# Weight loads issued from GpSimd's queue instead of SyncE's

## The chip, the cores and the metric

The kernel runs on one core of one Trainium2 chip. Five engines take part: TensorE (PE in the profile; PEld are its weight loads), VectorE (DVE), ScalarE (ACT), GpSimd (POOL) and SyncE (SP). Each has its own queue of instructions, worked off in order; semaphores tie the queues together. A transfer is issued by an instruction in one of these queues and then runs on the core's 16 DMA engines. The metric is the time of one execution on the device, in microseconds; lower is better.

## What is computed

One inference step of a one-layer streaming encoder, on 1024 prompt tokens and 8 x 16 sample tokens of width 1024, in fp32:

```
x = x + 0.5 * SwiGLU_1(RMSNorm(x))                 # 1024 -> 2816 -> 1024
z = RMSNorm(x) @ w_in                              # 1024 -> 2500 columns: q, k, v, indexer
A = differential attention, 4 heads                # softmax(q0 k0) - lam * softmax(q1 k1)
B = sparse attention, 8 heads, one shared key and value; an indexer picks the top 256 keys
x = x + concat(A, B) @ w_out
x = x + 0.5 * SwiGLU_2(RMSNorm(x))
```

Queries and keys are RMS-normalised by head. The outputs are x and the new keys and values of prompt and samples.

## The kernel before

**Tiling.** The nine tiles of 128 tokens form two groups: GA (prompt tiles 0 to 3 and the sample tile) and GB (prompt tiles 4 to 7). Each weight matrix is passed over once for each group. The stages in order of time are: FFN 1 of GA (from 26 us), FFN 1 of GB, with the norm and projection of GA in it (from about 510), the sample's attention and the attention of GA beside the rest of FFN 1 of GB (from about 710), out-projection of GA and projection of GB (from about 1376), FFN 2 of GA beside the attention of GB (from about 1590), out-projection of GB and its norm (from about 2265), and FFN 2 of GB alone (from about 2410).

**Weights.** The weights come in 160 loads of 1 MB (four of them 904 KB) into `raw`, a ring of `RAW = 2` slots. A gate or up load is 128 partitions x 8 x 256 floats, so 1024 pieces of 1 KB; a load of `w_in` or `w_out` is 512 pieces of 2 KB; one of `w_down` is 256 pieces of 4 KB. Each load is used as two units. ScalarE copies a unit to `w_hi` (L1452), rounded to the format of the fast matmul; DVE computes `w_lo = raw - w_hi` (L1735); both lie in rings of `HILO = 4`. TensorE multiplies three times (L1150 to L1152 for gate and up, L1167 to L1169 for down, L1187 to L1189 for the projections). `load(n)` waits until DVE has split the last unit of load n - 2 (`w_ready`), and its landing raises `raw_loaded`, which ScalarE's split waits for (named L2270 in the profile).

**The order.** `make_plan` writes one list of items by hand-set weights; every engine walks the whole list and issues its own part of each item. `Plan` puts `("load", n + 2)` right behind the split that frees the slot. So the order of each queue is fixed at build time.

**SyncE** issues every transfer: the loads; x tiles (`load_x`, L2277) and norm gains; the projection's results (`p_finish`, L2331), four stores a tile in its last column group; the key, query, value and bias tiles of attention (`k_store` L2383, `keys` L2395, `q_load` L2423, `near` L2415); attention rows for the out-projection (`o_load`, L2358), which wait until the buffer of two is free; and the outputs.

**GpSimd** does little: it writes constants at the start, then turns each sum of squares into a factor by two short operations, a scaled sum and a power of -0.5. These are `mean` and `rstd` for the norms (L2207, L2209; DVE's scaling into `rows`, L1811, waits for them), `p_mean` and `p_rstd` for the heads of a projection (L2216, L2218; DVE's `p_rows` waits), and `omean` and `orstd` for the heads of differential attention (L2228, L2230; DVE's `o_store` waits). It also clears some tiles with memsets (L2234, L2235). At the start, each x tile goes through ScalarE's square, GpSimd's two operations, DVE's `rows`, TensorE's transposes (L1207) and a copy and difference into `XTh` and `XTl`, before the first split.

Of the kernel before, what the change touches and what calls it, by code (L numbers as in the profile page):

```python
# [28 lines left out]
P = 128  # L29
D = 1024  # L30
KD = D // P
# [10 lines left out]
F_PAIR = 2  # L42
# [20 lines left out]
OUT_GROUP = 512  # L63
# [68 lines left out]
F_PAIR = 2  # L132
# [5 lines left out]
IN_GROUPS = -(-IN_COLS // OUT_GROUP)  # L138
TAIL = IN_COLS - (IN_GROUPS - 1) * OUT_GROUP
# [3 lines left out]
PAIRS = tuple((ffn, g, f) for ffn in range(2) for g in range(2) for f in range(N_PAIR))  # L143
HILO, RAW = 4, 2
# [573 lines left out]
def build(nc, io):  # L718
    plan = Plan()
# [11 lines left out]
    with ExitStack() as ctx:  # L731
# [12 lines left out]
        raw = sb("raw", [P, RAW, 2 * D])  # L744
# [9 lines left out]
        with ExitStack() as layout:  # L754
# [6 lines left out]
            with ExitStack() as shared:  # L761
# [4 lines left out]
                square = lay_s("square", [P, D], F16)  # L766
# [147 lines left out]
        w_ready = sem("w_ready")  # L914
# [215 lines left out]
        with nc.Block() as block:  # L1130
# [1062 lines left out]
            def _(pool):  # L2193
                order = Chain(pool, pool_chain)

                def start():
                    pool.memset(ident[:], 0.0).then_inc(ident_zero, 1)
                    pool.memset(mhalf[:], -0.5).then_inc(mhalf_set, 1)
                    pool.wait_ge(ident_zero, 1)
                    pool.affine_select(out=ident[:], in_=ident[:], compare_op=ALU.not_equal, fill=1.0, base=0,  # L2200
                                       pattern=[[-1, P]], channel_multiplier=1).then_inc(ident_ready, 1)
                    pool.wait_ge(mhalf_set, 1)

                def square_rows(tag, i):
# [32 lines left out]
                def x_norm(part):  # L2237
                    if part == 1:
# [3 lines left out]

                stages = {"start": start, "square": square_rows, "mm": mm, "near_zero": near_zero, "o_square": o_square,
                          "x_begin": x_begin, "x_norm": x_norm}
# [5 lines left out]
            def _(sp):  # L2250
                def load(n):
                    name = plan.loads[n]
                    if n >= RAW:
                        sp.wait_ge(w_ready, plan.load_end[n - RAW] + 1)
                    slot = raw[:, n % RAW]
                    if name[0] == "gu":
                        _, p, w = name
                        ffn, g, f = PAIRS[p]
                        src = (wu if w else wg)[ffn][:, :, f * F_PAIR * P:(f + 1) * F_PAIR * P]
                        dst = slot.rearrange("p (k n) -> p k n", k=KD)  # L2260
                    elif name[0] == "d":
                        ffn, g, f = PAIRS[name[1]]
                        src = wd[ffn][:, f * F_PAIR:(f + 1) * F_PAIR, :]
                        dst = slot.rearrange("p (k n) -> p k n", k=2)
                    else:
                        phase, g, cg, half = name
                        width = TAIL if phase == "P" and cg == IN_GROUPS - 1 else OUT_GROUP
                        src = (w_in if phase == "P" else w_out)[:, 4 * half:4 * half + 4, cg * OUT_GROUP:cg * OUT_GROUP + width]
                        dst = slot.rearrange("p (k n) -> p k n", k=4)[:, :, 0:width]
                    sp.dma_start(dst, src).then_inc(raw_loaded[n % RAW], 16)  # L2270

                def load_x(g, i):
# [6 lines left out]
                def start():  # L2279
# [3 lines left out]
                    load_x(GA, 2)  # L2283
                    load(0)
                    load_x(GA, 3)
                    load(1)
                    load_x(GA, 4)
# [223 lines left out]
                def past_sample():  # L2511
                    sp.wait_ge(s_stored, 32)
                    sp.sem_inc(fence, 1)

                stages = {"start": start, "load": load, "gain": gain, "tab": tab, "tab_store": tab_store, "p_finish": p_finish,
                          "spill": spill, "enter": enter, "reload": reload, "o_load": o_load, "down": down, "k_load": k_load,
# [45 lines left out]
```

## Time and profile before

| What | Value |
|---|---|
| Median of 3 runs | 2785.19 us (2785.16 to 2785.62) |
| The profiled execution | 2782.92 us, around a span of 2781.1 us |
| PE, DVE, ACT, POOL busy | 2553.6, 1456.4, 1061.2, 136.4 us |
| Granted TensorE clock, mean | 0.966 of full speed |
| Moved by DMA | 271.29 MB, 98 GB/s in the mean, all of the kernel's transfers on one queue (q1) |
| Weight loads | 160, 1024 KB each, about 5 us from issue to landing |

The profile shows one execution. "Idle before" is the time in which an engine had nothing running ahead of an instruction, and the arrow names what ended it. SPq rows are instructions that issue a transfer on SyncE; their duration is that of the issue, not that of the transfer. TensorE's matmuls overlap, so that the busy times of single rows add up to more than the stretch they stand in.

### The profile page before, as it was taken

The page shows a single profiled execution, that of the slowest core. Times are in us where ns is not written, and L with a number is a line of the kernel's source. Part 1 is how long each engine was busy: PE and PEld are TensorE (multiplying, and loading weights), DVE is VectorE, ACT ScalarE, POOL GpSimd, SP SyncE. Part 2 cuts the span into 40 slices and gives each one's busy share as a digit, 9 for nine tenths or more (in the row PEclk, how much of TensorE's full clock was granted, in tenths as well). Part 3 has the DMA queues.
Part 4 walks back from the last instruction along what each step waited for, and adds up shares of the span by engine and source line. Part 5 has one row for each costly group of instructions (what it writes and reads, how often), then busy time and mean ns, then how long its engine had stood idle before and what let it go on. Part 6 is the DMA issues. An engine that isn't in the chain of part 4 may idle for free.

```text
span 2781.1 us, 36356 instructions
## 1 busy us (share of the span) xinstructions
PE 2553.6 (92%) x13547; PEld 2181.6 (78%) x13547; DVE 1456.4 (52%) x2884; ACT 1061.2 (38%) x1821; POOL 136.4 (5%) x203
## 2 busy tenths in 40 slices
PE   7999999999899977878799997888899989999997
PEld 6899999888677666666688886778788878888886
DVE  4445444543454347875445358878755534444443
ACT  3132222332332235644334347775545532222221
POOL 0000000122000000000003100000000000000000
PEclk9999999999999998998899999999999999999998
DMA  5231221323533342222333442222112122322321
GB/s 179 78 119 62 90 76 61 137 102 122 156 129 112 99 137 89 86 72 76 118 122 120 156 128 70 72 79 79 59 47 64 56 94 99 114 91 95 103 91 61
DMA packets 244076, 271.29 MB, mean 98 GB/s; under 512 B 72096, under 2 KB 196544, under 8 KB 243904
## 3 DMA queue, kind: packets, MB, share of 16 engines
q1 hardware_dynamic: 243904, 268.98, 29.6%
q8 instruction: 110, 1.80, 0.3%
q14 instruction: 62, 0.51, 0.1%
HBM read 235.21 MB, written 35.29 MB: 97 GB/s over the span
## 4 chain that ended last, share of the span: by engine, by line
PE 70%; DVE 10%; issue 7%; ACT 7%; DMA 3%; SPq 1%; DVEq 0%; POOL 0%; ACTq 0%
PE bank L1150 10%; PE bank L1151 10%; PE bank L1152 10%; PE bank L1167 5%; PE bank L1168 5%; PE bank L1169 5%; PE bank L1187 4%; PE bank L1189 4%; PE bank L1188 4%; PE bank L1277 2%; ACT w_hi L1452 2%; DVE w_lo L1735 2%; PE bank L1412 1%; ACT junk_a_b L1609 1%; PE bank L1207 1%
## 5 line engine op out<-in xcount | busy, mean ns | idle before, releaser
L1735 DVE TENSOR_TENSOR w_lo<-raw,w_hi 128x1024 fp32r<-128x1024 f32 x320 | 385.8, 1219 | 194.1 <-ACT w_hi L1452 194.0
L1150 PE MATMUL bank<-XTh_a,w_hi 128*128 128x320 f32 x1408 | 449.1, 319 | 22.4 <-DVE act_in L1748 19.5
L1151 PE MATMUL bank<-XTl_a,w_hi 128*128 128x320 f32 x1408 | 441.1, 313 | 0.0
L1152 PE MATMUL bank<-XTh_a,w_lo 128*128 128x320 f32 x1408 | 441.0, 313 | 0.0
L1452 ACT ACTIVATE w_hi<-raw 128x1024 fp32r<-128x1024 f32 x320 | 330.1, 1046 | 171.1 <-PE bank L1189 105.7
L1167 PE MATMUL bank<-w_hi,hid_hi 128*128 128x512 f32 x792 | 325.2, 411 | 13.9 <-DVE X_a L1766 10.7
L1168 PE MATMUL bank<-w_lo,hid_hi 128*128 128x512 f32 x792 | 315.0, 398 | 0.0
L1169 PE MATMUL bank<-w_hi,hid_lo 128*128 128x512 f32 x792 | 313.8, 396 | 0.0
L1150 PEld LDWEIGHTS bank<-XTh_a,w_hi 128*128 128x128 f32 x1408 | 270.6, 192 | 34.9 <-issue 14.5
L1150 PE MATMUL bank<-XTh_b,w_hi 128*128 128x512 f32 x704 | 293.2, 416 | 0.0
L1151 PE MATMUL bank<-XTl_b,w_hi 128*128 128x512 f32 x704 | 284.0, 403 | 0.0
L1152 PE MATMUL bank<-XTh_b,w_lo 128*128 128x512 f32 x704 | 283.9, 403 | 0.0
L1766 DVE SCALAR_TENSOR_TENSOR X_a<-bank,X_a 128x512 f32<-128x512 f32 x220 | 151.6, 690 | 239.5 <-PE bank L1169 236.8
L1151 PEld LDWEIGHTS bank<-XTl_a,w_hi 128*128 128x128 f32 x1408 | 270.8, 192 | 5.3
L1152 PEld LDWEIGHTS bank<-XTh_a,w_lo 128*128 128x128 f32 x1408 | 270.0, 192 | 0.0
L1465 ACT ACTIVATE act_in<-bank 128x320 f32<-128x320 f32 (+1 forms) x132 | 64.8, 491 | 413.2 <-PE bank L1152 400.0
L1766 DVE SCALAR_TENSOR_TENSOR X_b<-bank,X_b 128x512 f32<-128x512 f32 x176 | 121.5, 691 | 179.0 <-PE bank L1169 175.8
L1470 ACT ACTIVATE hid_hi<-act_in 128x320 fp32r<-128x320 f32 (+1 forms) x132 | 69.1, 523 | 351.8 <-DVE act_in L1748 351.6
L1167 PEld LDWEIGHTS bank<-w_hi,hid_hi 128*128 128x128 f32 x792 | 151.1, 191 | 48.6 <-issue 20.8
L1169 PEld LDWEIGHTS bank<-w_hi,hid_lo 128*128 128x128 f32 x792 | 151.3, 191 | 34.6
L1168 PEld LDWEIGHTS bank<-w_lo,hid_hi 128*128 128x128 f32 x792 | 151.7, 192 | 25.5
L1152 PEld LDWEIGHTS bank<-XTh_b,w_lo 128*128 128x128 f32 x704 | 135.9, 193 | 33.6
(314 smaller groups left out, 3938.8 us busy)
## 6 DMA issues: line engine op xcount, KB each, us to landing
raw<-in_w_gate SPq DMA_DIRECT2D x44, 1024.0 KB, 5.0
raw<-in_w_up SPq DMA_DIRECT2D x44, 1024.0 KB, 5.0
raw<-in_w_down SPq DMA_DIRECT2D x44, 1024.0 KB, 4.8
raw<-in_w_in SPq DMA_DIRECT2D x16, 1024.0 KB, 4.8
s_k_in<-in_cache_diff_k SPq DMA_DIRECT2D x16, 512.0 KB, 4.7
s_v_in<-in_cache_diff_v SPq DMA_DIRECT2D x8, 1024.0 KB, 5.6
raw<-in_w_out SPq DMA_DIRECT2D x8, 1024.0 KB, 5.1
q_rows_b<-q_scr SPq DMA_DIRECT2D x80, 64.0 KB, 2.2
```

The source lines that it names most:

```text
L1150: pe.matmul(out, hi[:, k], XTh[g][:, k, lo:up], start=(k == 0), stop=False)
L1151: pe.matmul(out, hi[:, k], XTl[g][:, k, lo:up], start=False, stop=False)
L1152: last = pe.matmul(out, low[:, k], XTh[g][:, k, lo:up], start=False, stop=(k == KD - 1))
L1167: pe.matmul(out_of(key)[:], hid_hi[:, j, tok], hi[:, j], start=(j == 0), stop=False)
L1168: pe.matmul(out_of(key)[:], hid_hi[:, j, tok], low[:, j], start=False, stop=False)
L1169: last = pe.matmul(out_of(key)[:], hid_lo[:, j, tok], hi[:, j], start=False, stop=(j == F_PAIR - 1))
L1187: pe.matmul(out, XTh[g][:, k, tok], hi[:, e], start=(k == 0), stop=False)
L1188: pe.matmul(out, XTh[g][:, k, tok], low[:, e], start=False, stop=False)
L1189: last = pe.matmul(out, XTl[g][:, k, tok], hi[:, e], start=False, stop=(k == KD - 1))
L1452: act.activation(hilo(w_hi, u)[:, :, 0:width_of(u)], raw_part(u), ACT.Copy).then_inc(w_hi_ready, 1)
L1735: dve.tensor_tensor(hilo(w_lo, u)[:, :, 0:width_of(u)], raw_part(u), hilo(w_hi, u)[:, :, 0:width_of(u)].bitcast(F32), ALU.subtract).then_i ...
L1766: dve.scalar_tensor_tensor(x, out_of(key)[:], 0.5, x, ALU.mult, ALU.add).then_inc(frees(key), 1)
```

## The change

The function `load` and its 160 calls move from the SyncE program to the GpSimd program. Nothing else is changed: not the sizes, the semaphores, the ring of two slots or the places in the list of items. In GpSimd's `start`, loads 0 and 1 stand behind the constants; on SyncE they stood between the x tiles.

```diff
             @block.gpsimd
                 def start():
...
                     pool.wait_ge(mhalf_set, 1)
-
+                    load(0)
+                    load(1)
+
+                def load(n):
+                    name = plan.loads[n]
+                    if n >= RAW:
+                        pool.wait_ge(w_ready, plan.load_end[n - RAW] + 1)
+                    slot = raw[:, n % RAW]
...
+                    pool.dma_start(dst, src).then_inc(raw_loaded[n % RAW], 16)
...
+                stages = {"start": start, "load": load, "square": square_rows, "mm": mm, "near_zero": near_zero, "o_square": o_square,
             @block.sync
-                def load(n):
-                    name = plan.loads[n]
-                    if n >= RAW:
-                        sp.wait_ge(w_ready, plan.load_end[n - RAW] + 1)
...
-                    sp.dma_start(dst, src).then_inc(raw_loaded[n % RAW], 16)
...
                     load_x(GA, 2)
-                    load(0)
                     load_x(GA, 3)
-                    load(1)
                     load_x(GA, 4)
...
-                stages = {"start": start, "load": load, "gain": gain, "tab": tab, "tab_store": tab_store, "p_finish": p_finish,
+                stages = {"start": start, "gain": gain, "tab": tab, "tab_store": tab_store, "p_finish": p_finish,
```

GpSimd's queue at the end of the projection of GA, before (`p_mean` and `p_rstd` of the last column group for the last three of five tiles, then the two memsets of the sample's attention):

```order
L2216 TENSOR_SCALAR p_mean<-p_sum 128x1
L2218 TENSOR_TENSOR p_rstd<-p_mean,mhalf 128x1
L2216 TENSOR_SCALAR p_mean<-p_sum 128x1
L2218 TENSOR_TENSOR p_rstd<-p_mean,mhalf 128x1
L2234 MEMSET s_qi 128x512
L2235 MEMSET s_qm 128x1280
L2240 TENSOR_SCALAR s_ossum<-s_ossum 128x4
L2241 TENSOR_TENSOR s_orstd<-s_ossum,mhalf 128x4
```

And in the changed kernel:

```order
L2225 DMA raw<-in_w_up 128x8x256
L2239 TENSOR_SCALAR p_mean<-p_sum 128x1
L2241 TENSOR_TENSOR p_rstd<-p_mean,mhalf 128x1
L2239 TENSOR_SCALAR p_mean<-p_sum 128x1
L2241 TENSOR_TENSOR p_rstd<-p_mean,mhalf 128x1
L2239 TENSOR_SCALAR p_mean<-p_sum 128x1
L2241 TENSOR_TENSOR p_rstd<-p_mean,mhalf 128x1
L2225 DMA raw<-in_w_gate 128x8x256
L2257 MEMSET s_qi 128x512
L2258 MEMSET s_qm 128x1280
```

Two weight loads have come in between: one ahead of the third of the five pairs, one ahead of the memsets.

SyncE's queue before the out-projection of GB, before (`o_scr` is where attention leaves its rows, `rows` the buffer of two from which they are transposed, `x_scr` the stored x):

```order
L2270 DMA raw<-in_w_out 128x4x512
L2433 DMA o_scr<-o_b 128x128 x2
L2352 DMA X_b<-x_scr 128x1024 x4
L2358 DMA rows<-o_scr 128x1024 x3
L2270 DMA raw<-in_w_out 128x4x512
L2358 DMA rows<-o_scr 128x1024
L2270 DMA raw<-in_w_out 128x4x512
L2270 DMA raw<-in_w_gate 128x8x256
L2270 DMA raw<-in_w_down 128x2x1024
```

And in the changed kernel:

```order
L2433 DMA o_scr<-o_b 128x128 x6
L2352 DMA X_b<-x_scr 128x1024 x4
L2358 DMA rows<-o_scr 128x1024 x4
L2306 DMA gain_b<-in_g_ffn 128x1024
L2367 DMA out_y_p<-X_a 128x1024 x4
```

The loads of `w_out` have left the row, so the four transfers to `rows` now follow each other directly.

## Rows read from the trace of the kernel before

**Rows 1.** Page, parts 1 and 4: engines busy; chain that ended last.

```profile
PE 2553.6 (92%) x13547; PEld 2181.6 (78%) x13547; DVE 1456.4 (52%) x2884; ACT 1061.2 (38%) x1821; POOL 136.4 (5%) x203
...
PE 70%; DVE 10%; issue 7%; ACT 7%; DMA 3%; SPq 1%; DVEq 0%; POOL 0%; ACTq 0%
```

**Rows 2.** Tile `raw`: idle us, waits, what ended them; issue to landing.

```profile
  DMA raw<-in_w_down: 10.7, 1
...
DMA to landing us min/median/max: 4.4/5.0/11.1
```

**Rows 3.** Waits of SyncE's own queue: us in total, times, longest.

```profile
SPq L2270 <- DVE w_lo L1735: 1450.4, 152, 22.9
```

**Rows 4.** Timeline, last stage: start, us, engine and operation, [idle before].

```profile
2570.25 0.37 SPq L2270 DMA_DIRECT2D raw<-in_w_down  x1
2584.57 0.37 SPq L2270 DMA_DIRECT2D raw<-in_w_up  x1
...
2574.42 2.00 ACT L1452 ACTIVATE w_hi<-raw 128x1024 fp32r<-128x1024 f32 x2
...
2595.34 1.05 ACT L1452 ACTIVATE w_hi<-raw 128x1024 fp32r<-128x1024 f32 x1
...
2580.92 0.69 DVE L1748 TENSOR_TENSOR act_in<-act_in,bank 128x512 f32<-128x512 f32 x1 [2.64 <-PE bank L1152]
```

**Rows 5.** Groups of GpSimd: count, busy us, mean ns of one.

```profile
L2235 POOL MEMSET s_qm<- 128x1280 f32 x1 | 1.2, 1164 | 0.0
```

**Rows 6.** Timeline, end of the first projection: ScalarE, DVE, GpSimd, SyncE.

```profile
693.43 1.06 ACT L1452 ACTIVATE w_hi<-raw 128x1024 fp32r<-128x1024 f32 x1 [10.73 <-DMA raw<-in_w_down]
...
698.39 1.23 DVE L1735 TENSOR_TENSOR w_lo<-raw,w_hi 128x1024 fp32r<-128x1024 f32 x1 [0.73 <-ACT w_hi L1452]
...
700.30 0.19 POOL L2216 TENSOR_SCALAR p_mean<-p_sum 128x1 f32<-128x1 f32 x1 [1.72 <-DVE p_sum L1782]
...
700.11 0.55 SPq L2331 DMA_DIRECT2D out_sk_p<-p_rows  x1
700.69 0.43 SPq L2331 DMA_DIRECT2D out_sv_p<-p_rows  x1
```

**Rows 7.** Timeline, the start: GpSimd and DVE.

```profile
1.16 0.29 POOL L2200 TENSOR_SCALAR_AFFINE_SELECT ident<-ident 128x128 f32<-128x128 f32 x1 [0.20 <-POOL ident L2197]
...
5.69 0.19 POOL L2207 TENSOR_SCALAR mean<-ssum 128x1 f32<-128x1 f32 x1 [4.24 <-ACT square L1503]
...
19.83 1.28 DVE L1811 SCALAR_TENSOR_TENSOR rows<-X_a,rstd,gain_b 128x1024 f32<-128x1024 f32 x1
...
24.74 1.23 DVE L1735 TENSOR_TENSOR w_lo<-raw,w_hi 128x1024 fp32r<-128x1024 f32 x1 [0.25 <-ACT w_hi L1452]
```

**Rows 8.** Timeline near 2275: TensorE, SyncE; landing of the transfers to tile `rows`.

```profile
2273.09 1.47 PE L1207 MATMUL bank<-ident,rows 128*128 128x128 f32 x12
...
2282.16 1.12 PE L1207 MATMUL bank<-ident,rows 128*128 128x128 f32 x4 [7.60 <-DMA rows<-o_scr]
...
2276.46 0.51 SPq L2358 DMA_DIRECT2D rows<-o_scr  x1
...
DMA to landing us min/median/max: 3.1/5.7/9.5
```

**Rows 9.** Timeline, key stores of group A: DVE, SyncE, TensorE.

```profile
1021.04 0.69 DVE L1867 CAST k_out_a<-bank 128x512 fp32r<-128x512 f32 x1
...
1025.88 3.56 SPq L2383 DMA_DIRECT2D kT_scr<-k_out_a  x2
...
1038.81 0.69 PE L1246 MATMUL bank<-kT_a,q_hi_a 128*128 128x384 f32 x1 [8.64 <-DMA kT_a<-kT_scr]
```

**Rows 10.** Timeline near 1095: DVE and GpSimd.

```profile
1094.80 1.23 DVE L1735 TENSOR_TENSOR w_lo<-raw,w_hi 128x1024 fp32r<-128x1024 f32 x1 [0.26 <-ACT w_hi L1452]
1098.75 0.34 DVE L1979 SCALAR_TENSOR_TENSOR o_a<-o_a,orstd_a,sub_gain 128x128 f32<-128x128 f32 x1
...
1095.14 0.93 POOL L2228 TENSOR_SCALAR omean_a<-ossum_a 128x1 f32<-128x1 f32 x1 [10.16 <-ACT o_sq_a L1597]
```

More of the change, by code:

```diff
@@ L2202, in start @@
                     pool.wait_ge(mhalf_set, 1)
+                    load(0)
[5 more added lines that the diff above has]
+                    slot = raw[:, n % RAW]
+                    if name[0] == "gu":
+                        _, p, w = name
+                        ffn, g, f = PAIRS[p]
+                        src = (wu if w else wg)[ffn][:, :, f * F_PAIR * P:(f + 1) * F_PAIR * P]
+                        dst = slot.rearrange("p (k n) -> p k n", k=KD)
+                    elif name[0] == "d":
+                        ffn, g, f = PAIRS[name[1]]
+                        src = wd[ffn][:, f * F_PAIR:(f + 1) * F_PAIR, :]
+                        dst = slot.rearrange("p (k n) -> p k n", k=2)
+                    else:
+                        phase, g, cg, half = name
+                        width = TAIL if phase == "P" and cg == IN_GROUPS - 1 else OUT_GROUP
+                        src = (w_in if phase == "P" else w_out)[:, 4 * half:4 * half + 4, cg * OUT_GROUP:cg * OUT_GROUP + width]
+                        dst = slot.rearrange("p (k n) -> p k n", k=4)[:, :, 0:width]
+                    pool.dma_start(dst, src).then_inc(raw_loaded[n % RAW], 16)
                 def square_rows(tag, i):
@@ L2241, in x_norm @@
                         pool.tensor_tensor(s_orstd[:], s_ossum[:], mhalf[:, 0:DIFF_HEADS], ALU.pow).then_inc(s_orstd_ready, 1)
-                stages = {"start": start, "square": square_rows, "mm": mm, "near_zero": near_zero, "o_square": o_square,
+                stages = {"start": start, "load": load, "square": square_rows, "mm": mm, "near_zero": near_zero, "o_square": o_square,
                           "x_begin": x_begin, "x_norm": x_norm}
@@ L2250, in _ @@
             def _(sp):
-                def load(n):
-                    name = plan.loads[n]
-                    if n >= RAW:
-                        sp.wait_ge(w_ready, plan.load_end[n - RAW] + 1)
[L2255 to L2269, printed above, removed]
-                    sp.dma_start(dst, src).then_inc(raw_loaded[n % RAW], 16)
                 def load_x(g, i):
```

## The prediction

> **What bounds the kernel now.** I read the profile from the top down. TensorE is busy for 92% of the span and makes up 70% of the chain that ended last [rows 1]. DMA is 3% of that chain, the SyncE queue 1%, GpSimd almost nothing. So the kernel is bound by TensorE, and a change of queues can only move the 227 us (2781.1 - 2553.6) in which TensorE stands idle.
>
> The second view is the one of the weight tile: of all 320 splits that read `raw`, one waited for its transfer, for 10.7 us; a load lands 5.0 us after its issue in the median and 11.1 us at worst [rows 2]. The loads are prefetched well, and what they cost SyncE's queue is head-of-line time: the queue stood for 1450 us before weight loads, waiting for `w_lo` [rows 3]. Other transfers stand behind such a wait. GpSimd, which takes the loads over, is busy for 5% of the span [rows 1]. Its short operations feed DVE (`rstd`, `p_rstd`, `orstd`), and they will now stand behind loads in the same way.
>
> So there are three questions: which transfers come earlier on SyncE, which GpSimd operations come later, and whether a load issued by GpSimd lands late.
>
> **The unknown: what a load costs on GpSimd.** No DMA is issued there in this trace, so I bound the time g for which one gate or up load (1024 pieces of 1 KB) holds the engine. From below: SyncE issues it in 0.37 us [rows 4]. Above it, what is unknown is the work of listing the pieces: 1024 pieces with a source and a destination each are 2048 entries, and GpSimd's own memset takes 1.16 us for 1280 columns, 0.91 ns a column [rows 5]; at one column's time an entry that is 1.9 us. As the upper end I take four columns' time an entry, 7.5 us. I take g = 2 us, because a memset is the nearest row of work that only writes; half of it for `w_in` and `w_out` (512 pieces), a quarter for `w_down` (256). A gain below 0.37 us is excluded, since SyncE's issue writes nothing itself. The landing moves by about as much: +2 us for gate and up, +0.5 us for `w_down`, if the list is finished before the data moves; 0 to +7.5 us at the ends.
>
> **Late landing.** The tightest loads are the `w_down` of the last stage. One is issued at 2570.25, lands about 5 us later, and ScalarE splits it as the second of two `w_hi` from 2574.42 [rows 4], so at 2575.4: under half a microsecond of room, at some ten places. Behind it DVE has 2.64 us of idle time before its product at 2580.92 [rows 4], so +0.5 us is hidden, and up to about 3 us would be. The next up load is issued at 2584.57 and split at 2595.34 [rows 4], 10.8 us later, so it may land 5.8 us late. Cost: 0. The one landing that was waited for is the `w_down` split at 693.43 [rows 6], in the tail of a projection; there +0.5 us goes through at worst. If g is 7.5, it is 1.9 us.
>
> A rule of the Trainium skill speaks against the change (page "DMA: Bandwidth & Descriptors", section "Measured (HBM→SBUF, 128 partitions, SWDGE, issued from GpSimd)"): 1 MB issued from GpSimd keeps the DMA engines 6.15 us, whereas the whole way from issue to landing is 5.0 us here [rows 2]. By it every landing would come one to two microseconds later still, and the sum would stay, because the room named above is 3 us.
>
> **The start.** Now the five x tiles and two weight loads share one queue, and the first `w_lo` starts at 24.74 [rows 7]. With the loads elsewhere, issued from 1.45 (the end of `affine_select`, [rows 7]), GpSimd is blocked until S = 1.45 + 2g. Its first `mean` runs at 5.69, so g = 2 (S = 5.45) delays nothing. From S on, the chain needs 0.85 us for mean and power, 1 us to the first `rows`, five tiles at 2.66 us of DVE (1.28 for `rows` [rows 7], about 0.69 for each of two `XTl`), and about 2 us of latency: 17.2 us. At g = 2 it is done by 22.6 instead of 24.5: gain 1.9 us if the tiles come early enough, which they should, for 2 of the 5 MB ahead of the last one leave its queue, though not the DMA engines. Bounds: +10 us cost at g = 7.5 (S = 16.5, done by 33.7, minus 24.5), 3 us gain below.
>
> **SyncE freed.** Three places matter. (a) The last load of attention rows for group B. TensorE does twelve transposes from 2273.09; the fourth frees the buffer by about 2273.6. SyncE stands before a `w_out` load and issues `rows` right behind it, at 2276.46 [rows 8], with its 1 MB ahead; TensorE waits 7.60 us for it, until 2282.16 [rows 8]. In the changed kernel it is issued 2.9 us earlier and lands in about 3.1 us, the best of its group, instead of 5.7 [rows 8]. Gain 2.9 to 5.5 us; I take 5, as the weight load then starts only when the rows have landed. (b) The key stores of group A: the part whose cast starts at 1021.04 is stored only at 1025.88, right behind a weight load, and TensorE waits 8.64 us at 1038.81 for what follows [rows 9]. The last part is ready only at about 1026 anyway, so only bandwidth is gained: 0 to 3 us, taken as 1. (c) Elsewhere (query rows behind a gate load near 1038, the store burst at 700 to 710 with two loads of 0.4 us in it, rows behind `w_out` near 1388) single waits of 2 us or so shrink: 0 to 3 us, taken as 1.5. Sum 9.4 us.
>
> A second page rule is weighed here. The Trainium skill, same page, section "Issuing engines are not separate DMA queues", says that issuing from several engines saves only the sequencer's time, as all run on the same 16 DMA engines. The row at 2276.46 speaks for more: there the queue's order, not the issue, costs 2.9 us. By the rule the sum would lose the landing part of (a) and all of (b), about 3 us.
>
> **GpSimd's own operations.** Every one that stands behind a load in the new order is delayed by g plus the remaining wait for `w_lo`; what counts is when DVE needs the result. Near 700 the last three `p_mean` stand behind an up load that is ready at 699.6, when `w_lo` from 698.39 ends; the first ran at 700.30 and would start at 701.6 [rows 6]. DVE is 1.3 us late. But SyncE stores these tiles from 700.11 on, four transfers of about 0.5 us each a tile [rows 6], and reaches the third tile at about 704, when its data is 2.5 us old: no cost. Near 1095 DVE's `w_lo` ends at 1096.03, so `orstd` is ready at 1096.8 + g; DVE uses it at 1098.75 [rows 10]. That leaves 1.9 us: cost g - 1.9. There are four more such places (`orstd` near 1108, 1164 and 1772, `rstd` near 2344), with 1.6 to 4 us of room. At g = 2 they sum to about 1.5 us, and I add 0.3 for the split at 693.43 and small stalls. At g = 5 they cost 4 + 3 + 3 + 2 + 3.4 = 15 us.
>
> **Sum.** -9.4 + 1.8 = -7.6 us against the profiled execution (2782.92 us around a span of 2781.1). The median of the three runs is 2785.19, 2.3 us above that execution; so 2785.2 - 7.6 = 2777.6, about **2778 us**.
>
> **Rivals.**
> 1. *Listing the pieces is slow and GpSimd becomes a gate.* Same mechanism with g = 5: the start costs S = 11.45, done by 28.7, so 4.2 us instead of a gain of 1.9; the delayed results cost 15; the load split at 693.43 and small stalls 1.5 to 3; the up loads of the last stage land 5 us late and have 5.8. The gains of SyncE stay at 7.5. Net +15: 2800 us. It decides from g = 3.4, where costs equal gains. For it: 1024 small pieces a load. Against it: GpSimd is nearly empty. At g = 7.5 it is 2825.
> 2. *GpSimd and DVE get in each other's way.* The `omean` at 1095.14 took 0.93 us while DVE ran `w_lo`, and the `mean` at 5.69 took 0.19 [rows 7, 10]; so the two do disturb each other where both read SBUF. If a load's issue waits for DVE or holds it for its 2 us, 160 loads meet DVE in half of the cases (it is busy 52%, [rows 1]); with TensorE covering three quarters of that, it costs 160 x 0.5 x 2 x 0.25 = 40 us: 2818 us. The Trainium skill (page "SBUF — State Buffer", section "Who interferes with whom") says that DVE's `tensor_tensor` takes only the read side of the shared ports, and that descriptors need the write side; by that this rival falls.
> 3. *It does nothing:* the same bytes on the same DMA engines, loads that nobody waits for, and the freed places are caught by the next wait (the chain near 1038 and 2282 has other feeders). 2785 us.
> 4. *All gains at their ends, g near 0.4:* -3 - 5.5 - 3 - 3 = -14.5: 2771 us.
>
> **Chances.** Forecast 0.42, rival 1 0.28, rival 2 0.08, rival 3 0.14, rival 4 0.08. A measurement of this kernel tells 0.2% (5.6 us) from no change, so faster means below 2779.6. The forecast's own spread of 4 us puts about 0.27 of its 0.42 below that and 0.15 within; rival 4 is all faster; rival 3 and a fifth of rival 1 are within. That makes 0.35 faster, 0.35 same and 0.30 slower. The range runs from rival 4 to g of about 6.5: 2771 to 2815.
>
> **What would show each step.** `DMA` rows of GpSimd with g in them, against 2 us. The first `w_lo` at about 22.8. TensorE's wait of 7.60 us before the rows near 2282 falls to about 2.5. SyncE's waits for `w_lo` are gone, and GpSimd has them. The wait for `raw` stays near one. If DVE shows new waits for `orstd`, `p_rstd` or `rstd`, rival 1 holds; if `w_lo` itself takes longer than 1.22 us, rival 2. The forecast is wrong if g is over 3.4, or if the waits at 1038 and 2282 stay.

## The result, and the profile after

The changed kernel is faster, by more than forecast: 2769.03 us in the median of five runs (2766.69 to 2772.28), beside 2785.16 us for the kernel before (2782.32 to 2785.62, five runs). The ratio is 0.9944, 95% interval 0.9930 to 0.9959. The prediction was 2778 us with a range of 2771 to 2815; the measured time lies 2 us below it. The profiled execution took 2766.69 us around a span of 2764.1, so 17.0 us less than the one of before.

The first lines of the page (busy time and share of each engine, then the chain that ended last) and part 3 of the page (queues: packets, MB, share of the 16 engines):

```profile
PE 2545.1 (92%) x13547; PEld 2174.5 (79%) x13547; DVE 1456.3 (53%) x2884; ACT 1061.6 (38%) x1821; POOL 268.0 (10%) x363
...
q0 software_dynamic: 43200, 167.29, 17.4%
q1 hardware_dynamic: 125632, 101.69, 11.5%
...
PE 70%; DVE 10%; issue 7%; ACT 7%; DMA 3%; SPq 1%; POOL 0%; DVEq 0%; ACTq 0%
```

TensorE's busy time fell from 2553.6 [rows 1] to 2545.1, by 8.5 us, with the same 13547 matmuls. The idle time fell from 227.5 to 219.0 us (span minus busy), also by 8.5. So half of the gain between these two traces is no waiting time at all: the same matmuls spent less time at the lower granted clock. The mean granted clock of the changed kernel's five executions is 0.968 to 0.972, 0.970 in the mean, beside 0.966 for 21 executions of the kernel before. (The 0.972 of the profiled one reads too high: at the start its trace gives 1.00 where the matmuls run as slowly as before, 0.47 us for 320 columns.) The prediction has no term for the clock.

The second view is GpSimd's: its groups of instructions (line, operation, tiles, count | busy us, mean ns of one), and the longest of its waits (us, times, longest).

```profile
L2225 POOL DMA_DIRECT2D raw<-in_w_up x44 | 40.7, 924 | 778.1 <-DVE w_lo L1735 778.1
L2225 POOL DMA_DIRECT2D raw<-in_w_gate x44 | 39.6, 901 | 317.7 <-DVE w_lo L1735 317.5 <-issue 0.2
L2225 POOL DMA_DIRECT2D raw<-in_w_down x44 | 31.9, 724 | 627.2 <-DVE w_lo L1735 627.2
```

```profile
POOL raw L2225 <- DVE w_lo L1735: 2013.8, 157, 38.0
```

A load holds GpSimd for 0.9 us (gate and up) or 0.7 us (`w_down`), where g was taken as 2 us. SyncE's 1450 us of waiting for `w_lo` [rows 3] are gone, and GpSimd waits instead. The tile view of `raw`, on who waited for its transfer and on landing times:

```profile
  DMA raw<-in_w_down: 13.7, 7
...
DMA to landing us min/median/max: 4.9/5.5/15.4
```

A load lands 5.5 us after its issue, not 5.0 [rows 2]. Seven splits waited for a transfer where it was one, for 13.7 us in all instead of 10.7.

Now the places. At the start (GpSimd, then DVE, then ScalarE's square of the last x tile; start, us, operation, [idle before]):

```profile
1.70 1.03 POOL L2225 DMA_DIRECT2D raw<-in_w_gate  x1 [0.24 <-issue]
2.73 0.89 POOL L2225 DMA_DIRECT2D raw<-in_w_up  x1
```

```profile
8.48 2.48 DVE L1811 SCALAR_TENSOR_TENSOR rows<-X_a,rstd,gain_b 128x1024 f32<-128x1024 f32 x2 [6.58 <-DMA gain_b<-in_g_ffn]
...
24.22 4.63 DVE L1735 TENSOR_TENSOR w_lo<-raw,w_hi 128x1024 fp32r<-128x1024 f32 x4 [0.25 <-ACT w_hi L1452]
```

```profile
16.44 1.06 ACT L1503 ACTIVATE square<-X_a 128x1024 bf16<-128x1024 f32 x1 [0.57 <-DMA X_a<-in_x_sample]
```

In the kernel before, the same square:

```profile
16.96 1.06 ACT L1503 ACTIVATE square<-X_a 128x1024 bf16<-128x1024 f32 x1 [1.89 <-DMA X_a<-in_x_sample]
```

The first `w_lo` starts at 24.22 instead of 24.74 [rows 7]. The last x tile is issued at 3.07 instead of 5.31, but it lands only 0.5 us earlier. Before the last attention rows (SyncE, then TensorE), and TensorE's row in the table of stretches for the 4 us behind that wait (busy and count of PE, PEld, DVE, ACT, POOL; clock; DMA share; GB/s):

```profile
2265.20 0.32 SPq L2358 DMA_DIRECT2D rows<-o_scr  x1
```

```profile
2268.51 1.09 PE L1207 MATMUL bank<-ident,rows 128*128 128x128 f32 x8 [2.47 <-DMA rows<-o_scr]
```

```profile
2268.00:2272.00 4.00, 3.49 (x26) 3.49 (x27) 3.44 (x6) 1.09 (x2) 0.51 (x1) 1.00 0.97 327
```

The wait is 2.47 us instead of 7.60 [rows 8], and the clock stays at 1.00. In the kernel before, the stretch behind the same wait reads 0.50, the lower of the two levels (1.2 GHz):

```profile
2282.00:2286.00 4.00, 3.84 (x16) 3.84 (x17) 1.38 (x2) 1.19 (x2) 0.00 (x0) 0.50 0.00 0
```

At the key stores of group A (SyncE, TensorE):

```profile
1019.87 4.60 SPq L2383 DMA_DIRECT2D kT_scr<-k_out_a  x2
```

```profile
1032.71 0.69 PE L1246 MATMUL bank<-kT_a,q_hi_a 128*128 128x384 f32 x1 [4.46 <-DMA kT_a<-kT_scr]
```

The wait of 8.64 us [rows 9] is 4.46. The kernel before has a second one behind it, for query rows, which the changed kernel has not:

```profile
1046.38 0.44 PE L1232 MATMUL bank<-ident,q_rows_a 128*128 128x128 f32 x2 [2.14 <-DMA q_rows_a<-q_scr]
```

The same place of group B is worse than before (GpSimd, SyncE, TensorE):

```profile
1600.60 0.92 POOL L2225 DMA_DIRECT2D raw<-in_w_up  x1 [22.66 <-DVE w_lo L1735]
```

```profile
1600.96 2.21 SPq L2383 DMA_DIRECT2D kT_scr<-k_out_b  x2
```

```profile
1616.84 0.47 PE L1246 MATMUL bank<-kT_b,q_hi_b 128*128 128x128 f32 x1 [9.10 <-DMA kT_b<-kT_scr]
```

TensorE waits 9.10 us here, 5.82 in the kernel before, whose SyncE issued the same load and the same two stores so:

```profile
1610.22 0.38 SPq L2270 DMA_DIRECT2D raw<-in_w_up  x1
1610.85 3.22 SPq L2383 DMA_DIRECT2D kT_scr<-k_out_b  x2
...
1624.74 0.48 PE L1246 MATMUL bank<-kT_b,q_hi_b 128*128 128x128 f32 x1 [5.82 <-DMA kT_b<-kT_scr]
```

The landing times of tile `kT_scr`, for group A (issues of 1020 to 1030 in the kernel before, of 1015 to 1026 in the changed one), then for group B (1610 to 1615 before, 1600 to 1604 changed):

```profile
DMA to landing us min/median/max: 8.3/8.9/9.5
```

```profile
DMA to landing us min/median/max: 3.3/3.4/3.5
```

```profile
DMA to landing us min/median/max: 7.4/7.9/8.4
```

```profile
DMA to landing us min/median/max: 9.3/9.5/9.7
```

In group A the stores now get away before the weight load and land in 3.4 us. In group B the load stood just ahead of two stores in the kernel before (by 0.6 us) and still does (by 0.4 us), now on the other queue: the stores land after 9.5 us instead of 7.9, so the queue of its own does not shield them. DVE's cast that makes these stores ready starts at 1600.22 instead of 1610.11, so 9.9 us earlier; TensorE's first matmul on the keys starts only 7.9 us earlier. These 2.0 us are what the transfers cost more than before. At 1600, however, TensorE was 12.4 us ahead of the kernel before. The other 2.5 us of that lead the cast never shared.

The two traces hold the same matmuls in the same order. The lead of the changed kernel at a given matmul is its start before minus its start after, and how it grows over a stretch is what that stretch gained. The table has this for the changed kernel and for experiments of the next section (each against the same trace of the kernel before):

```
                         lead gained, us, from..to (time in the kernel before)
                         start   keys A         keys B         last rows      all
                         ..26.0  1020.3..1060.2 1600.2..1660.0 2265.1..2300.1 ..2768.1
changed kernel            0.5     7.5           -4.4            6.6           17.0
e1 five loads on GpSimd   0.0     7.4           -1.9            6.9           14.2
e2 the other 155          1.5     0.9           -4.0            0.3           -1.1
e11 SyncE waits again     1.1     3.8           -3.9            2.9            0.6
e4 hold                   1.4     8.9            1.4            5.8           20.1
e3 order alone           -0.1    11.0            4.9            6.0           24.6
e5 w_out load later       0.1    -0.5            1.7            6.7            9.7
e6 two loads of A later   0.0    11.1           -0.6            0.1           11.3
```

Stretches whose code an experiment leaves alone show the scatter of one trace: up to 1.7 us in the table (e5, keys B), and from 26 to 1020, which the table leaves out, e3, e5 and e6 lost 2.0 to 2.5 us.

### The profile page after: what moved, and what is told of

It is laid out like the page before. It is cut to its first block, busy times and chain, and to the rows that moved or that the text cites. A ratio compares the mean times of both kernels' runs of the same rounds, so it can differ in the third digit from the quotient of the medians.

```text
span 2764.1 us, 36355 instructions
## 1 busy us (share of the span) xinstructions
PE 2545.1 (92%) x13547; PEld 2174.5 (79%) x13547; DVE 1456.3 (53%) x2884; ACT 1061.6 (38%) x1821; POOL 268.0 (10%) x363
## 3 DMA queue, kind: packets, MB, share of 16 engines
q0 software_dynamic: 43200, 167.29, 17.4%
q1 hardware_dynamic: 125632, 101.69, 11.5%
## 4 chain that ended last, share of the span: by engine, by line
PE 70%; DVE 10%; issue 7%; ACT 7%; DMA 3%; SPq 1%; POOL 0%; DVEq 0%; ACTq 0%
PE bank L1150 10%; PE bank L1151 10%; PE bank L1152 10%; PE bank L1167 5%; PE bank L1168 5%; PE bank L1169 5%; PE bank L1187 4%; PE bank L1189 4%; PE bank L1188 4%; PE bank L1277 2%; ACT w_hi L1452 2%; DVE w_lo L1735 2%; PE bank L1412 1%; ACT junk_a_b L1609 1%; PE bank L1369 1%
## 5 line engine op out<-in xcount | busy, mean ns | idle before, releaser
L1735 DVE TENSOR_TENSOR w_lo<-raw,w_hi 128x1024 fp32r<-128x1024 f32 x320 | 386.2, 1219 | 194.6 <-ACT w_hi L1452 194.4
L1167 PE MATMUL bank<-w_hi,hid_hi 128*128 128x512 f32 x792 | 324.4, 410 | 13.2 <-DVE X_a L1766 10.7
```

What stands on the lines that cost most here:

```text
L1167: pe.matmul(out_of(key)[:], hid_hi[:, j, tok], hi[:, j], start=(j == 0), stop=False)
L1735: dve.tensor_tensor(hilo(w_lo, u)[:, :, 0:width_of(u)], raw_part(u), hilo(w_hi, u)[:, :, 0:width_of(u)].bitcast(F32), ALU.subtract).then_i ...
```

## The experiments

The kernel before was run beside each of three groups of experiments and took 2781.79, 2781.29 and 2784.53 us. So ratios are compared, and the time of its own group stands behind "before" each time.

### Is it a few places, or all 160 loads?

e1 issues five loads from GpSimd: 62 and 63 (group A), 94 and 95 (group B), which stand between key stores, keys and query rows, and 121, which stands before the last attention rows. e2 is the complement. The loads of either queue count on semaphores of their own.

```diff
+    ON_POOL = {62, 63, 94, 95, 121}          # e2: set(range(160)) - {62, 63, 94, 95, 121}
...
                 def load(n):                  # in the GpSimd program
+                    if n not in ON_POOL:
+                        return
...
                 def load(n):                  # in the SyncE program
+                    if n in ON_POOL:
+                        return
```

> The kernel before, with five of its 160 loads issued from GpSimd: the two up and two gate loads that stand between the key stores, key loads and query rows at the opening of either group's attention (numbers 62, 63, 94, 95), and the w_out load in front of the last attention rows (121). The other 155 stay on SyncE. Theory (the gain is the place of a few loads in SyncE's queue): the key chain of group A starts as early as in the changed kernel, TensorE's wait of 8.64 us at 1038.81 falls to about 4.5, the wait of 7.60 us at 2282.16 goes, together 13 us of the 17: 2772 us. In group B the stores still run into an up load on the shared DMA engines, so nothing is gained there. Rival (the gain is spread: smaller issue cost on SyncE, fewer and larger packets for all 160 loads): 5 of 160 loads move a thirtieth of it: 2784 us.

Measured: 2769.70 us (2768.87 to 2770.95), before 2781.79; ratio 0.9955 (0.9942 to 0.9967).

> The complement: those five loads stay where they were in SyncE's queue, the other 155 are issued from GpSimd. Theory: the waits of TensorE at the opening of group A's attention (8.64 us) and before the last attention rows (7.60 us) stay; what is left is the start (0.5 us) and single small stalls: 2781 us. Rival (spread gain): nearly all of it, 2769 us.

Measured: 2785.65 us (2781.97 to 2790.02), before 2781.79; ratio 1.0016 (1.0007 to 1.0025). TensorE's waits for keys and for rows, in e2's timeline:

```profile
1036.48 0.69 PE L1248 MATMUL bank<-kT_a,q_hi_a 128*128 128x384 f32 x1 [10.08 <-DMA kT_a<-kT_scr]
...
2283.39 0.90 PE L1209 MATMUL bank<-ident,rows 128*128 128x128 f32 x3 [7.62 <-DMA rows<-o_scr]
```

Five loads bring 12 of the 16 us. The other 155 bring nothing, and the interval says that they cost a little, some 4 us. By the table e2 loses 4.0 us at the keys of B, where its loads are on SyncE as before: it came there 3.1 us ahead, the key stores were issued no earlier than before, and the lead was gone. The two parts together (0.9955 x 1.0016 = 0.9971) are less than the whole (0.9944); what the remaining 0.27% are stays open. The theory of places stands, the rival of a spread gain falls.

### Each place by itself, without GpSimd

e5 and e6 keep all loads on SyncE and only move them in its order. A load item is skipped in the walk through the plan and issued behind another item:

```diff
+                moved = {("load", 121): ("o_load", "otb", 3)}      # e5
+                moved = {("load", 62): ("q_load", 4), ("load", 63): ("q_load", 6)}      # e6
                 for item in plan.items:
-                    if item[0] in stages:
+                    if item[0] in stages and item not in moved:
                         stages[item[0]](*item[1:])
+                    for load_item, anchor in moved.items():
+                        if item == anchor:
+                            load(load_item[1])
```

> The kernel before; in SyncE's order the w_out load 121 stands behind the last attention rows instead of in front of them, nothing else. Theory (the 17 us are three places, each by itself): TensorE's wait of 7.60 us at 2282.16 shrinks to about 2, and the clock, which fell to 0.50 behind that wait, stays at 1.00, worth 1.5 us more: 2.9 + 4 us, about 6.5 in all, 2775 us beside 2782 for before. Rival (the earlier rows only move the wait to the next feeder): under 2 us, 2780.

Measured: 2774.37 us (2771.14 to 2780.15), before 2781.29; ratio 0.9979 (0.9970 to 0.9988). The page's first line and the wait:

```profile
PE 2548.7 (92%) x13547; PEld 2177.5 (79%) x13547; DVE 1455.4 (53%) x2884; ACT 1060.9 (38%) x1821; POOL 136.6 (5%) x203
```

```profile
2275.87 1.09 PE L1207 MATMUL bank<-ident,rows 128*128 128x128 f32 x8 [2.44 <-DMA rows<-o_scr]
```

> The kernel before; only loads 62 and 63 stand later in SyncE's order, behind the query rows of block 4 and of block 6 of group A. Theory: TensorE's 8.64 us at 1038.81 fall to 4 or less and the query rows at 1046.38 are no longer late: 8 to 9 us, 2773 us beside 2782 for before. Rival (the term of my prediction was right, 1 us for the bandwidth and some for the rows; the rest came from elsewhere): 2 to 3 us, 2779.

Measured: 2772.75 us (2771.65 to 2775.79), before 2781.29; ratio 0.9970 (0.9960 to 0.9981).

```profile
1034.73 0.44 PE L1246 MATMUL bank<-kT_a,q_hi_a 128*128 128x384 f32 x1 [2.08 <-DMA kT_a<-kT_scr]
```

Both came out as the theory had them, 7 and 8.5 us. Each place pays by itself. e5 moved one instruction: its wait shrank by 5.2 us, and its stretch gained 6.7. Part of the rest is the clock: behind the wait it is granted 1.00 (2275 to 2283), where the kernel before reads 0.50.

### The order alone, all three places

e3 moves the same five loads as e1, but in SyncE's order (94 behind `("q_load", 40)`, 95 behind `("q_load", 42)`).

> No load on GpSimd. The same five loads stay on SyncE, only later in its order: the up load behind all key stores, key loads and query rows of block 4, the gate load behind the query rows of block 6 (in both groups), the w_out load behind the last attention rows. Theory (order alone is enough, and it also keeps the 1 MB off the DMA engines while the keys travel): the gain of e1, and in group B more, as the key stores there no longer land after 8 us but after 3.5, and TensorE's 5.82 us at 1624.74 shrink to about 2: 2766 us, faster than the changed kernel. Rival (a queue of their own is what helps, since urgent transfers then don't line up behind 1 MB in one ring): order alone gives only the earlier issue, 2780 us.

Measured: 2758.15 us (2756.96 to 2763.80), before 2781.79; ratio 0.9917 (0.9903 to 0.9930). TensorE at the keys of A, of B, and at the last rows:

```profile
1034.41 0.45 PE L1246 MATMUL bank<-kT_a,q_hi_a 128*128 128x384 f32 x1 [2.15 <-DMA kT_a<-kT_scr]
...
1608.78 0.48 PE L1246 MATMUL bank<-kT_b,q_hi_b 128*128 128x128 f32 x1 [2.06 <-DMA kT_b<-kT_scr]
...
2259.37 0.88 PE L1207 MATMUL bank<-ident,rows 128*128 128x128 f32 x6 [2.42 <-DMA rows<-o_scr]
```

No queue of their own was needed, and by the two ratios (0.9917 and 0.9944) the result is 0.27%, 7.5 us, better than the changed kernel. Group B's keys gain 4.9 us where the changed kernel lost 4.4. The rival (a ring of their own helps) falls.

### Is it the load beside the key stores?

e4 is the changed kernel in which loads 62 and 94 wait longer, until the first three key transfers of their group have landed:

```diff
                 def load(n):                  # in the GpSimd program
...
+                    if n in (62, 94):
+                        m = 2 if n == 62 else 12
+                        pool.wait_ge(keys_loaded[m % K_RING], keys_in[m])
```

> The changed kernel, where GpSimd's loads 62 and 94 (with 63 and 95 queued behind them) also wait until the first three rows of keys of the group have landed. Theory (what is left in the changed kernel is the load's 1 MB on the same 16 DMA engines beside the key stores: 9.66 and 9.27 us to landing in group B against 3.36 and 3.51 in group A): TensorE's wait of 9.10 us at 1616.84 falls to about 3, the one at 1032.71 from 4.5 to about 2.5: 2761 us. Rival (the stores of group B are slow because of their own traffic, 1 MB of rows and values ahead of them): no change, 2769 us.

Measured: 2761.43 us (2758.87 to 2762.84), before 2781.79; ratio 0.9924 (0.9911 to 0.9936). Landing of the two key stores of group B (issues of 1602 to 1606), and TensorE:

```profile
DMA to landing us min/median/max: 3.3/4.0/4.6
```

```profile
1612.86 0.48 PE L1246 MATMUL bank<-kT_b,q_hi_b 128*128 128x128 f32 x1 [3.28 <-DMA kT_b<-kT_scr]
```

The two stores land after 3.3 and 4.6 us instead of 9.7 and 9.3, and TensorE waits 3.28 us instead of 9.10. The forecast of 2761 was met. What held the stores up in group B was the load's 1 MB on the DMA engines at their moment; group B gains 1.4 us here where the changed kernel lost 4.4. Loads 62 and 94 were issued 9.8 and 13.7 us later than they could have been, and still landed 10 and 8 us before their first use.

### The wait in SyncE's queue, or the 1 MB in its ring?

e11 is the changed kernel; SyncE waits again for `w_lo` wherever a load stood, and issues nothing.

```diff
             @block.sync
+                def load(n):
+                    if n >= RAW:
+                        sp.wait_ge(w_ready, plan.load_end[n - RAW] + 1)
...
-                stages = {"start": start, "gain": gain,
+                stages = {"start": start, "load": load, "gain": gain,
```

> The changed kernel, but SyncE still waits for w_lo at each place where a load stood, and issues nothing there. It parts the two things that the change takes from SyncE's queue: the wait in front of other transfers, and the 1 MB ahead of them in one ring. Theory (the wait is the larger part near the last attention rows: it is held from 2273.6 to 2276.0; at the key stores the first store again comes 4 us late, and then runs beside the load): the 6.6 us of the last rows shrink to 2, the 8 us of group A's keys to 3: 2779 us. Rival (it is the shared ring, behind whose 1 MB the rows line up): most of the gain stays, 2771.

Measured: 2781.70 us (2778.97 to 2784.36), before 2784.53; ratio 0.9991 (0.9982 to 1.0000). SyncE and TensorE before the last rows:

```profile
2278.52 0.32 SPq L2358 DMA_DIRECT2D rows<-o_scr  x1
```

```profile
2281.83 1.97 PE L1207 MATMUL bank<-ident,rows 128*128 128x128 f32 x8 [4.77 <-DMA rows<-o_scr]
```

Of the 16 us, 3 are left. It is the wait in front of other transfers that the change took away. What stands ahead of the rows matters too: they are issued late again, but 0.27 us ahead of GpSimd's `w_out` load (2278.79) and not 0.43 us behind it. They land in 3.3 us, so TensorE waits 4.77 us and not 7.60, and that stretch keeps 2.9 of its 6.6 us.

### The cost side: a longer hold of GpSimd

e7 and e12 put work behind each load on GpSimd, on a small tile of its own (three powers, or one). The load is not later, GpSimd's other results are.

```diff
                     pool.dma_start(dst, src).then_inc(raw_loaded[n % RAW], 16)
+                    for _ in range(REPS):      # 3 in e7, 1 in e12
+                        order.link(pool.tensor_tensor(spin[:], spin[:], mhalf[:], ALU.pow))
```

> The changed kernel, where GpSimd computes three powers of a small tile of its own behind each load (about 1.5 us each), so that a load holds it for 5.5 us instead of 0.9, while the load itself is not later. It measures the cost side of the prediction, which had the delayed results cost 15 us at g = 5 and the start 4 instead of a gain of 2. Theory (the costs were sized rightly, only g was not): 15 to 22 us above the changed kernel, 2786 us. Rival (the waits for GpSimd's results were priced too high, since DVE has other work in the gap): under 8 us, 2776.

Measured: 2815.24 us (2814.19 to 2816.09), before 2781.29; ratio 1.0121 (1.0106 to 1.0137). The added work took 1.70 us each, so the hold was 0.9 + 5.1 = 6.0 us. DVE's waits for GpSimd (us, times, longest):

```profile
DVE p_rows L1797 <- POOL p_rstd L2246: 39.0, 29, 6.1
DVE rows L1813 <- POOL rstd L2237: 28.2, 8, 13.5
DVE o_a L1981 <- POOL orstd_a L2258: 21.2, 8, 5.1
```

> As e7, with one power behind each load instead of three: a load holds GpSimd for 2.6 us. Without it the changed kernel took 2769 us, with three 2815 (46 us for 5.2 us of hold). Theory (places have different room, 1.6 to 4 us, so that the first two microseconds of hold are nearly free and the cost rises later, as in the prediction): 2774 us. Rival (cost in proportion): 2784 us.

Measured: 2780.89 us (2776.97 to 2783.39), before 2784.53; ratio 0.9985 (0.9976 to 0.9994).

Both expectations missed, on the same side; e12 lies nearer to its rival. The hold costs from the start: from 0.9944 (hold 0.9) to 0.9985 (2.6) and 1.0121 (6.0), that is 0.24% and then 0.40% for each microsecond, or 6.7 and 11 us. The five places with 1.6 to 4 us of room were not all that pay. In the changed kernel DVE waits for `p_rstd` for 26.0 us, 2.1 at most, where before it was 25.3, and for `orstd` for 1.5. e7 adds 13 us to the first and 26 to the second, and has 28.2 us for `rstd` in eight places; e12 has 9.0 us for `rstd` in three. Of the 50 us between the traces of e7 and of the changed kernel, 24 arise from 1060 to 1600, and 5.4 at the start. By these three points the gain is used up at a hold of about 3.0 us; the prediction had 3.4.

### More of the same order, and GpSimd on top

e8 has e3's order, and in addition loads 0 and 1 behind all x tiles of group A, load 51 behind the sample's first rows, load 78 behind the third attention rows of group A, and each group's reload of X behind its first two attention rows. e9 puts the reloads behind the fourth and third rows and load 78 behind the fifth. e10 is e9 with the 151 loads that were not moved on GpSimd.

```diff
+                moved = {("reload", 0): ("o_load", "ota", 1), ("reload", 1): ("o_load", "otb", 1),   # e9: 3, 2
+                         ("load", 62): ("q_load", 4), ("load", 63): ("q_load", 6), ("load", 94): ("q_load", 40),
+                         ("load", 95): ("q_load", 42), ("load", 121): ("o_load", "otb", 3),
+                         ("load", 51): ("x_new_load", 1), ("load", 78): ("o_load", "ota", 2)}   # e9: 4
...
                     load_x(GA, 2)
-                    load(0)
                     load_x(GA, 3)
-                    load(1)
                     load_x(GA, 4)
+                    load(0)
+                    load(1)
```

> All loads on SyncE, with the order of e3 and more of the same: the first two loads behind all five x tiles of group A; the gate load 51 behind the first rows and keys of the sample stage; the w_out load 78 behind the third attention rows of group A; the reload of X (5 and 4 transfers of 512 KB) behind the first two attention rows of each group instead of in front of them. Theory (every large transfer in front of one that TensorE waits for costs its own time on the DMA engines): start 2 to 3 us, sample stage 2, TensorE's waits for rows of 9.45 and 6.04 us down by 5 and 3: 12 us below e3, 2746 us. Rival (X is needed as soon as the rows, and the start is bound by the gain vector): 2755 us.

Measured: 2748.39 us (2746.02 to 2750.82), before 2781.29; ratio 0.9882 (0.9869 to 0.9896). This is the fastest of all, 1.2% below the kernel before, with no transfer on GpSimd. By the same comparison of matmuls as in the table it gained 3.7 us at the start, 11.2 and 5.1 at the keys and 6.9 at the last rows, 36.4 in all. Beyond e3, most of that is the start and the first attention rows of group B, for which the reload of X no longer stands ahead. TensorE and the rows of group A:

```profile
1361.65 1.09 PE L1207 MATMUL bank<-ident,rows 128*128 128x128 f32 x8 [1.52 <-DMA rows<-o_scr]
1371.69 1.12 PE L1207 MATMUL bank<-ident,rows 128*128 128x128 f32 x4 [6.68 <-DMA rows<-o_scr]
1379.07 0.66 PE L1207 MATMUL bank<-ident,rows 128*128 128x128 f32 x4 [1.05 <-DMA rows<-o_scr]
```

> All loads on SyncE, as in e8, but the reload of X stands behind the fourth attention rows of group A and the third of group B, and the w_out load 78 behind the fifth rows. In e8 the wait for the first rows of group A went, and 6 of the 8 us gained there were given back when the third to fifth rows landed after 9 to 10 us, with the reload and load 78 beside them. Theory: they are kept: 2742 us. Rival (X is now late for the sums that need it): 2750.

Measured: 2752.27 us (2749.40 to 2754.11), before 2784.53; ratio 0.9885 (0.9871 to 0.9898). Not better than e8: the rival. The reload only moved its collision to the next rows. In group A that changed little, 8.2 us of waits beside 9.3:

```profile
1362.23 1.09 PE L1207 MATMUL bank<-ident,rows 128*128 128x128 f32 x8 [1.70 <-DMA rows<-o_scr]
1366.54 0.66 PE L1207 MATMUL bank<-ident,rows 128*128 128x128 f32 x4 [0.93 <-DMA rows<-o_scr]
1369.64 0.66 PE L1207 MATMUL bank<-ident,rows 128*128 128x128 f32 x4 [0.63 <-DMA rows<-o_scr]
1377.09 1.11 PE L1207 MATMUL bank<-ident,rows 128*128 128x128 f32 x4 [4.97 <-DMA rows<-o_scr]
```

In group B the reload now stands ahead of the last rows, and the stretch "last rows" gains 2.1 us instead of 6.9. TensorE there in e9, then in e8:

```profile
2250.29 1.11 PE L1207 MATMUL bank<-ident,rows 128*128 128x128 f32 x4 [6.18 <-DMA rows<-o_scr]
```

```profile
2245.01 3.21 PE L1207 MATMUL bank<-ident,rows 128*128 128x128 f32 x16 [2.50 <-DMA rows<-o_scr]
```

My reason for it (X needed too soon) was wrong: the wait is for rows again.

> The order of e9, with the nine loads that were moved (0, 1, 51, 62, 63, 78, 94, 95, 121) on SyncE and the other 151 on GpSimd. Theory (GpSimd's queue brings nothing of its own; the bytes share the same DMA engines, landings are 0.5 us later, and SyncE's other waits matter nowhere): 2742 to 2747, level with e9 or a little slower, as e2 was with the kernel before. Rival (SyncE's waits for w_lo still hold single transfers, which then come out): 2737.

Measured: 2754.65 us (2753.57 to 2756.11), before 2784.53; ratio 0.9894 (0.9879 to 0.9909). The intervals of e9 and e10 overlap almost fully. With the order right, GpSimd's queue has nothing left to give.

## Why the prediction was right and wrong, point by point

**What bounds the kernel.** Right: TensorE; a change of queues works on its waits. Wrong was the next sentence, that it can *only* move the 227 us of idle time. TensorE's busy time moved as much as its idle time, 8.5 us each. The rows at 2282 and 2268 show one case of it: 0.50 of full clock behind a wait of 7.60 us, 1.00 behind one of 2.47. In e3 busy time is 2544.4 us, in e2 it is 2556.6. By the stretches of the table, busy time fell by 1.2 us at the keys of A and by 1.5 at the last rows, and rose by 0.9 at the start; 3.3 of the fall lie between the keys of A and of B. The rest was not tied to a wait. 1.6 of it are one stretch near 2757, where the trace before reads 0.50 (2757 to 2760) and the changed one, at the same matmuls, 1.00; e3 and e5 show that gain and e1 and e6 do not, so it is scatter.

**The cost of a load on GpSimd.** g was 0.9 us, not 2: mis-sized, but inside the bounds (0.37 to 7.5). I took the row of a memset as the nearest, at one column's time for each of 2048 entries. 1024 pieces took 0.90 us and 256 took 0.70, so that the count hardly matters. The landing moved by 0.5 us instead of 2.

**Late landing.** Right in its result (0): seven splits waited, 13.7 us of ScalarE, but TensorE's lead did not shrink in the last stage (15.4 us at 2300.1, 17.0 at the end). The rule from the Trainium skill (page "DMA: Bandwidth & Descriptors", section "Measured (HBM→SBUF, 128 partitions, SWDGE, issued from GpSimd)"), weighed there, keeps the DMA engines busy for 6.15 us with 1 MB from GpSimd; here the whole way to landing took 5.5 us in the median, 4.9 at least, so the measurement is below the rule.

**The start.** -1.9 forecast, -0.5 measured. GpSimd was free at 3.62 and cost nothing; the step that failed was "if the x tiles come early enough". The two loads shared the DMA engines with x tiles and gain vector: DVE's first `rows` started at 8.48 instead of 7.53, and the last x tile, issued 2.2 us earlier, landed 0.5 us earlier. e8, where the loads stand behind the x tiles, gained 3.7. The bounds were loose as well: the chain cannot start before `mean` at 5.69, so by these figures the gain is at most 1.7 us at any g, not 1.9 or 3, and the cost at g = 7.5 is 9.2 us, not 10.

**(a) The last attention rows.** Right mechanism: 5 us forecast, 6.6 measured, 5.1 of them in the wait and the rest the clock behind it. e5 has it with one instruction moved.

**(b) The key stores of group A.** This is the term of the sum that failed: 1 us forecast. The stretch gained 7.5: 4.2 in the wait for the keys, which is (b) itself, 1.9 where the wait of 2.14 us for query rows is gone, and 1.4 behind that, where the clock reads 1.00 (1038.9 to 1043) and in the kernel before 0.69 (1045 to 1050). The last two belong to (c), which had 1.5 for all of its places. I saw that the last part is ready only at about 1026 and concluded that only bandwidth was to be gained. But the transfer beside the load was the price: two stores took 8.9 us to land behind the load and 3.4 us ahead of it, and all keys wait for the last store. The rows to read were the landings of the stores near 1025, and I had taken none.

**Group B's keys.** Not foreseen: +4.4 us. I read group A's place only. In group B the split that releases the load and the cast that makes the stores ready follow each other on DVE in both kernels (`w_lo` from 1608.96, cast from 1610.11), so the load stays just ahead of the stores whichever queue it is on, and only the order in e3 or the hold in e4 parts them. In group A the last store got away 0.26 us ahead of the load (1024.11 and 1024.37), which nothing in the kernel ensures; in e11 a store issued the same 0.26 us ahead took 7.6 us to land. That part of the gain is luck.

**GpSimd's own operations.** +1.8 forecast, nothing measured, since g was 0.9. With g = 2.6 the longer hold costs 11 us (e12 beside the changed kernel): my five places were not the whole list. In e7 `p_rstd`, which the prediction put at "no cost", and `rstd` pay too.

**The rest.** Start, keys and last rows add up to 0.5 + 7.5 - 4.4 + 6.6 = 10.2 us of the 17.0. The other 6.8 lie between the places: 1.4 before the keys of A, 3.0 between those of A and of B (e3 and e6 have 3.3 and 3.5 there), 0.8 before the last rows and 1.6 behind them, the scatter near 2757. e1 shows 1.8 in these stretches, e2 0.2. The 3.0 are no term of the prediction and stay open. So the sum fell short because (b), and with it (c), was sized too small and the clock had no term; the +4.4 of group B hid part of that.

**Rivals.** Rival 1 (GpSimd as a gate) did not happen, but its mechanism is real and its turning point was nearly right (3.4, measured 3.0); beyond that it is steeper than I had it. Rival 2 (GpSimd and DVE disturb each other) fell: `w_lo` takes 1219 ns in both pages. Rival 3 (nothing happens) is true of 155 of the 160 loads. Rival 4 had the nearest time, 2771, for nearly the right reason, and too small a chance: its price for (b) was 3 us, where 4.2 were measured, and its start gave 0.5 and not 3.

**The page's rule.** The Trainium skill (same page, section "Issuing engines are not separate DMA queues") says that issuing from several engines saves the sequencer's time only, as all share 16 DMA engines. Group B shows just that: 9.5 us to landing with the load on the other queue, 7.9 with it on the same one, 3.3 and 4.6 with it held back in e4. What I held against it, that a queue's order is worth more than its issue time, stands too: 2.9 us of wait for one instruction, and e11, where the waits alone take back 13 of 16 us.

## What to carry to other kernels

Look for short transfers that someone waits for, and read what stands ahead of them in their queue, also when it only waits: a prefetch with room to spare (8 to 10 us were left even in e4) must not stand before them, nor start within the few microseconds in which they travel. Moving the bulk to another queue removes the first harm and leaves the second to chance; moving nine prefetches and two reloads later in the same queue put most of both right, cost nothing, and gave twice as much here (0.9882 beside 0.9944). And price a wait of TensorE with the stretch behind it, at the clock which its rows show.

## What the runs showed of the hardware

- A transfer of 1 MB holds GpSimd for 0.70 us at 256 pieces of 4 KB, 0.75 to 0.82 at 512 of 2 KB and 0.90 at 1024 of 1 KB, against 0.37 us on SyncE. I had expected a cost for each piece.
- The same loads moved in fewer packets from GpSimd: 167.29 MB in 43200 packets, 3.9 KB each, where the kernel before had 243904 packets for 268.98 MB in all. The changed kernel's SyncE queue has 125632, so the loads had taken 118272 packets there. They were no faster for it (5.5 us to landing).
- SyncE's issue itself can stall. Behind the weight load near 1025 the two key stores took 3.56 us to issue [rows 9], one of them 2.92, where an unhindered one takes 0.38.
